# The last block's feed-forward network takes x times the norm weight with two shift columns, and applies the root mean square behind the products

## The reference

```
x   = x + g1x * y_x
hx2 = _modulate(_rms_norm(x, norm2_g[l]), sh2x, sc2x)      # x*rsqrt(mean x^2)*g*(1+sc) + sh
a, val = _split(hx2 @ w_up, (2816, 2816))
a   = conv_3x3(a as an image of 4 rows x 64 columns, each channel by itself, 'SAME') + conv_b
x   = x + g2x * ((gelu(a) * val) @ w_down)
out = rms_norm(x, final_norm_g)
```

## Time and profile before

| | us |
|---|---|
| median of 3 runs | 1181.13 (1180.99 to 1182.02) |
| the profiled execution's own time | 1182.99 |
| its span, first to last instruction | 1181.7 |
| PE busy | 1149.7 (97%) |
| DVE busy | 832.6 (70%) |
| ACT busy | 617.5 (52%) |
| POOL busy | 149.0 (13%) |
| mean granted clock of PE | 0.988 of 2.4 GHz |

### The profile page before, as it was taken

One profiled execution on the slowest core, in us unless ns is written; L12 is line 12 of the kernel. 1 busy time (PEld: TensorE's weight loads), 2 busy tenths in 40 slices (PEclk: granted clock), 3 DMA queues, 4 the chain that ended last, 5 costly groups with the idle time before them and its releaser, 6 DMA issues.

```text
span 1181.7 us, 21814 instructions
## 1 busy us (share of the span) xinstructions
PE 1149.7 (97%) x8998; PEld 1103.4 (93%) x8998; DVE 832.6 (70%) x1291; ACT 617.5 (52%) x933; POOL 149.0 (13%) x111
## 2 busy tenths in 40 slices
PE   7999899999999999999999999999999989999996
PEld 6989899999998899999999798988999979999995
DVE  5767588878685766777777775677546767767775
ACT  5655544445566645444444754755447455555553
POOL 0002101010100002100100000000000032444441
PEclk9999999999999999999999999999999989999998
DMA  8645478776534344888888545354235543555540
GB/s 313 230 144 178 155 245 295 242 258 197 164 122 160 125 161 134 289 289 270 283 264 274 198 128 172 120 166 161 92 107 176 180 161 126 179 182 178 193 143 36
DMA packets 60322, 221.36 MB, mean 187 GB/s; under 512 B 6736, under 2 KB 6992, under 8 KB 59840
## 3 DMA queue, kind: packets, MB, share of 16 engines
q1 hardware_dynamic: 59760, 218.53, 55.6%
q10 hardware_dynamic: 288, 1.05, 0.3%
q0 software_dynamic: 176, 0.39, 0.1%
HBM read 218.90 MB, written 1.05 MB: 186 GB/s over the span
## 4 chain that ended last, share of the span: by engine, by line
PE 90%; DVE 5%; ACT 3%; issue 1%; DMA 1%; SPq 0%; POOL 0%; ACTq 0%; DVEq 0%
PE PS L359 25%; PE PS L361 24%; PE PS L360 24%; PE PS L364 15%; ACT w_hi L850 2%; DVE w_lo L1330 1%; DVE PS L1928 1%; DMA ARENA<-memT 1%; DVE H_lo L1373 0%; PE PS L613 0%; ACT ARENA L947 0%; DVE SQ L1363 0%; DVE ARENA L1956 0%; DVE ARENA L1363 0%; DVE ARENA L1432 0%
## 5 line engine op out<-in xcount | busy, mean ns | idle before, releaser
L1330 DVE TENSOR_TENSOR w_lo<-raw,w_hi 128x1024 fp32r<-128x1024 f32 x325 | 398.1, 1227 | 176.5 <-ACT w_hi L850 175.8
L850 ACT ACTIVATE w_hi<-raw 128x1024 fp32r<-128x1024 f32 x356 | 371.9, 1054 | 149.3 <-PE PS L361 123.3
L359 PE MATMUL PS<-Y_hi,w_hi 128*128 128x256 f32 x1240 | 358.6, 289 | 9.9 <-DVE Y_lo L1369 3.2
L360 PE MATMUL PS<-Y_lo,w_hi 128*128 128x256 f32 x1240 | 353.9, 285 | 0.0
L361 PE MATMUL PS<-Y_hi,w_lo 128*128 128x256 f32 x1240 | 353.6, 285 | 0.0
L359 PEld LDWEIGHTS PS<-Y_hi,w_hi 128*128 128x128 f32 x1240 | 239.3, 193 | 17.2 <-issue 8.5
L360 PEld LDWEIGHTS PS<-Y_lo,w_hi 128*128 128x128 f32 x1240 | 239.9, 193 | 0.4 <-issue 0.2
L361 PEld LDWEIGHTS PS<-Y_hi,w_lo 128*128 128x128 f32 x1240 | 239.7, 193 | 0.0
L359 PE MATMUL PS<-H_hi,w_hi 128*128 128x256 f32 x768 | 220.2, 287 | 3.4 <-issue 1.0
L360 PE MATMUL PS<-H_lo,w_hi 128*128 128x256 f32 x768 | 217.3, 283 | 0.0
L361 PE MATMUL PS<-H_hi,w_lo 128*128 128x256 f32 x768 | 217.2, 283 | 0.0
(11 more groups left out here) (233 smaller groups left out, 1361.4 us busy)
## 6 DMA issues: line engine op xcount, KB each, us to landing
raw<-stream SPq DMA_DIRECT2D x404, 512.0 KB, 4.2
ARENA<-memT SPq DMA_DIRECT2D x2, 512.0 KB, 7.6
X<-xT SPq DMA_DIRECT2D x1, 1024.0 KB, 11.3
ARENA<-ctxT SPq DMA_DIRECT2D x1, 1024.0 KB, 5.8
ARENA<-memT SPq DMA_DIRECT2D x1, 1024.0 KB, 7.4
outT<-ARENA SPq DMA_DIRECT2D x2, 512.0 KB, 2.6
CROW<-c_rows SPq DMA_DIRECT2D x1, 512.0 KB, 10.0
ARENA<-c_rows SPq DMA_DIRECT2D x1, 512.0 KB, 13.2
```

Source lines behind the costliest of these rows:

```text
L359: pe.matmul(o, wh, xh, start=start, stop=False, skip_group_check=True)
L360: pe.matmul(o, wh, xl, start=False, stop=False, skip_group_check=True)
L850: act.activation(w_hi[n % RING][:], raw[at][:], ACT.Copy).then_inc(*mark("hi", n))
L1330: dve.tensor_tensor(w_lo[n % RING][:], raw[raw_of("slot", n)][:], w_hi[n % RING][:], ALU.subtract).then_inc(*mark("lo_dve", n))
```

## The change

- The pair (X times gain) is now written during w_o2, into new tiles U_hi and U_lo of 8 chunks x 258 columns, which lie in memory that other tiles of the arena used earlier. Columns 256 and 257 of each chunk hold the shift sh, split into hi and lo before w_o2 begins (`shift_hi`, `shift_lo`).
- Gate and up products of the last block are 258 columns wide. Column 256 is sh @ W.
- `residual_sum(2)` moves from between w_o2 and gate(0) into gate(0), ahead of its chunk 6. The normed pair H2 of this place goes (8 times L1363, L883, L1369).
- A new DVE step `scaled(j, i)` multiplies each gate (i = 0) and up (i = 1) product by RS in place and copies the shift's product from column 256 into a column SHIFTED. The image is written by Identity with that column as bias. `conv_mid` reads the image in place of PSUM. `conv_value` becomes (product + column) * gelu in one instruction.
- The order on ACT becomes: gelu of j-1; `img`, `conv_mid` of j; `hidden` of j-1; the fills. On DVE: `scaled(j, 0)`; `conv_value` of j-1; taps of j; `hidden_low` of j-1; fill; `scaled(j, 1)`; fill; third fill.
- The zeroing of the images moves ahead of w_o2.

```diff
-            project("w_o2", KC, Y2, ...)
-            residual_sum(2)
+            pe.wait_ge(*past("shift_lo"))
+            conv_gate_up(0, [("h_lo", 2, k) for k in range(KC)], lambda: residual_sum(2))
...
-                tall(PS[:, 2 * p, 0:T], H2, ready)
+                tall(PS[:, 2 * p, 0:T + 2], (U_hi, U_lo), ready, within)
...
-                tall(PS[:, 2 * p + 1, 0:T], H2)
+                tall(PS[:, 2 * p + 1, 0:T + 2], (U_hi, U_lo))
```

On ACT:

```diff
-            project("w_o2", KC, left, then=residual_square(2))
+            act.wait_ge(*past("gs", 2))
+            act.wait_ge(*past("mod", 3))
+            act.activation(U_hi[:, :, T:T + 2], SH2_COLS, ACT.Copy).then_inc(*mark("shift_hi"))
+            project("w_o2", KC, left, then=residual_square(2, U_TOKENS, lambda c: GS[:, 2, c:c + 1]))
             inverse_rms("res2")
-            whole(norm_his("norm2", H2, lambda c: SH2(c)))
             act.preload_act_table(ACT.Gelu)
...
                 act.wait_ge(*past("used", gate_slot(2, j)))
+                act.wait_ge(*past("scaled", j, 0))
+                act.wait_ge(*past("bias", j, 0))
                 act.wait_ge(*past("taps", j - 2, 7) if j > 1 else past("img_zero"))
-                act.activation(IMGS[:, j % 2, 1:ROWS + 1, 1:COLS + 1], img, ACT.Copy).then_inc(*mark("img", j))
-                act.activation(conv_sum(j), img, ACT.Identity, bias=gain("fconv_b", j),
+                act.activation(inner, img, ACT.Identity, bias=bias).then_inc(*mark("img", j))
+                act.wait_ge(*past("img", j))
+                act.activation(conv_sum(j), inner, ACT.Identity, bias=gain("fconv_b", j),
...
             for j in range(FC):
+                if j:
+                    conv_value(j - 1)
                 conv_gate(j)
                 if j:
-                    conv_value(j - 1)
+                    hidden(2, j - 1)
                 fill()
                 fill()
-                if j:
-                    hidden(2, j - 1)
```

On DVE:

```diff
-            project("w_o2", KC, residual(2, lambda c: G1(c)))
+            dve.memset(IMGS, 0.0).then_inc(*mark("img_zero"))
...
+            dve.tensor_tensor(U_lo[:, :, T:T + 2], SH2_COLS, U_hi[:, :, T:T + 2],
+                              ALU.subtract).then_inc(*mark("shift_lo"))
+            project("w_o2", KC, residual(2, lambda c: G1(c)),
+                    then=residual_low(2, U_TOKENS, lambda c: GS[:, 2, c:c + 1]))
+
+            def scaled(j, i):
+                half = PS[:, 2 * (j % 2) + i, 0:T]
+                dve.wait_ge(*past("used", gate_slot(2, j) + i))
+                dve.tensor_tensor(half, half, RS[:, 0], ALU.mult).then_inc(*mark("scaled", j, i))
+                at = 2 * i + j % 2
+                dve.tensor_copy(SHIFTED[:, at:at + 1], PS[:, 2 * (j % 2) + i, T:T + 1]).then_inc(*mark("bias", j, i))
...
-                dve.tensor_tensor(up_product(j), PS[:, 2 * (j % 2) + 1, 0:T], GF[:],
-                                  ALU.mult).then_inc(*mark("hidden", 2, j))
+                dve.scalar_tensor_tensor(up_product(j), PS[:, 2 * (j % 2) + 1, 0:T],
+                                         SHIFTED[:, 2 + j % 2:3 + j % 2], GF[:], ALU.add,
+                                         ALU.mult).then_inc(*mark("hidden", 2, j))
+            dve.wait_ge(*past("rs", "res2"))
             for j in range(FC):
+                scaled(j, 0)
                 if j:
                     conv_value(j - 1)
-                fill()
                 conv_taps(j)
-                fill()
                 if j:
                     hidden_low(2, j - 1)
+                fill()
+                scaled(j, 1)
+                fill()
```

More of the change, by code:

```diff
@@ L107 @@
     "conv_act": ("img", "conv_mid"),
+    "shift_dve": ("shift_lo", "scaled", "bias"),
     "gates_act": ("vs_gelu", "u_gelu", "sig_r", "sig_a", "sig_b"),
@@ L234, in build @@
         CX = (CX_hi, CX_lo)
-        sb("above", [P, 24832 - 19584])
+        U_lo, U_hi = sb("U_lo", [P, KC, T + 2], F32R), sb("U_hi", [P, KC, T + 2], F32R)
+        sb("above", [P, 24832 - 19584 - 2 * KC * (T + 2)])
         def area(at, *shape):
@@ L290, in build @@
         RS_COLS = small[:, 32:34]
+        SHIFTED = small[:, 0:4]
+        SH2_COLS = MOD[:, 24:32, 0:1].to_broadcast([P, KC, 2])
+        U_TOKENS = (U_hi[:, :, 0:T], U_lo[:, :, 0:T])
         RS_OF = {"mem0": RS[:, 1], "mix0": RS[:, 0], "mix1": RS[:, 0], "ctx": LR[:, 1], "out": RS[:, 0]}
@@ L813, in pe_program, with conv_gate_up @@
             project("w_o2", KC, Y2, lambda i: ("added", 2, i), None, [("merged_lo", i) for i in range(KC)])
-            residual_sum(2)
-            def conv_gate_up(j, ready=None):
+            def conv_gate_up(j, ready=None, within=None):
                 p = j % 2
@@ L1291, in conv_gate @@
                 img = PS[:, b, 0:T].rearrange("p (r c) -> p r c", r=ROWS)
+                inner = IMGS[:, j % 2, 1:ROWS + 1, 1:COLS + 1]
+                bias = SHIFTED[:, j % 2:j % 2 + 1]
                 act.wait_ge(*past("used", gate_slot(2, j)))
+                act.wait_ge(*past("scaled", j, 0))
+                act.wait_ge(*past("bias", j, 0))
                 act.wait_ge(*past("taps", j - 2, 7) if j > 1 else past("img_zero"))
-                act.activation(IMGS[:, j % 2, 1:ROWS + 1, 1:COLS + 1], img, ACT.Copy).then_inc(*mark("img", j))
-                act.activation(conv_sum(j), img, ACT.Identity, bias=gain("fconv_b", j),
+                act.activation(inner, img, ACT.Identity, bias=bias).then_inc(*mark("img", j))
+                act.wait_ge(*past("img", j))
+                act.activation(conv_sum(j), inner, ACT.Identity, bias=gain("fconv_b", j),
                                scale=gain("fconv", j + 4 * FC)).then_inc(*mark("conv_mid", j))
@@ L1916, in dve_program @@
             project("br_b", KC, branch_b, then=merged_low)
-            project("w_o2", KC, residual(2, lambda c: G1(c)))
+            dve.memset(IMGS, 0.0).then_inc(*mark("img_zero"))
             dve.wait_ge(*past("gs", 2))
-            whole(norms("norm2", X, lambda c: GS[:, 2, c:c + 1], ("res2", RS[:, 0]), H2, lambda c: SH2(c)))
-            dve.memset(IMGS, 0.0).then_inc(*mark("img_zero"))
+            dve.wait_ge(*past("mod", 3))
+            dve.wait_ge(*past("shift_hi"))
+            dve.tensor_tensor(U_lo[:, :, T:T + 2], SH2_COLS, U_hi[:, :, T:T + 2],
[8 more added lines that the diff above has]
+                dve.tensor_copy(SHIFTED[:, at:at + 1], PS[:, 2 * (j % 2) + i, T:T + 1]).then_inc(*mark("bias", j, i))
             def conv_taps(j):
@@ L1933, in conv_value @@
                 dve.wait_ge(*past("gelu", j))
-                dve.wait_ge(*past("used", up_slot(2, j)))
-                dve.tensor_tensor(up_product(j), PS[:, 2 * (j % 2) + 1, 0:T], GF[:],
-                                  ALU.mult).then_inc(*mark("hidden", 2, j))
+                dve.wait_ge(*past("bias", j, 1))
+                dve.wait_ge(*past("scaled", j, 1))
+                dve.scalar_tensor_tensor(up_product(j), PS[:, 2 * (j % 2) + 1, 0:T],
+                                         SHIFTED[:, 2 + j % 2:3 + j % 2], GF[:], ALU.add,
+                                         ALU.mult).then_inc(*mark("hidden", 2, j))
+            dve.wait_ge(*past("rs", "res2"))
             for j in range(FC):
+                scaled(j, 0)
                 if j:
                     conv_value(j - 1)
-                fill()
                 conv_taps(j)
-                fill()
                 if j:
                     hidden_low(2, j - 1)
+                fill()
+                scaled(j, 1)
+                fill()
                 if j > 1:
```

1 line of the change is left out of this document (removed).

## The result

The changed kernel takes 1184.09 us (median of 15 runs, 1182.2 to 1186.2), the kernel before 1181.13 us (15 runs, 1180.65 to 1183.07). The ratio is 1.0024 with a 95% interval of 1.0017 to 1.0031: about 3 us slower, where 1173.8 us and a gain of 7.3 were predicted. The profiled execution of the changed kernel took 1182.2 us and is the fastest of its 15, that of before took 1182.99 and is above its median. So in the two traces the changed kernel is the faster one by 0.8 us, 3.75 us away from what the medians say, and I compare stretches within a trace, not spans (1180.9 and 1181.7 us).

The account below looks back on a forecast made before the run. PE's rate was taken to bound the last stage, with the start of up(2) deciding. The terms -8.33 + 0.83 + 0.17 = -7.3 us took 1181.13 to 1173.8 us, range 1171.5 to 1177.2.

Parts of the forecast that it names:

- The passage from w_o2 into ffn2: From the end of w_o2 to up(2): up(2) starts at 982.10 in place of 990.43, 8.33 us sooner.
- The table load: Gelu table load before turn 0's image: 1.30 us by the row; a page drain of 1.38 would cut the gain 1.4.
- The stall at up(2) stays and the clock falls: At up(2), PE still stalls 3.06 us for the low part of G(0); the lower clock again costs 1.38 us.
- The clock stays up in the stall: Rival, 12%: the clock does not fall at the up(2) stall, 1.4 us less, 1172.4 us.
- So it holds, with 1.0 us to spare in a pair: Even flow of ffn2: 16.3 us of DVE work in a pair of turns that lasts PE 17.4 us.
- VectorE becomes the bound: Rival, 10%: in ffn2, dearer DVE work and fills beside POOL's make a pair 0.4 us longer: 3.8 us, 1177.6 us.
- My price from the row of layer 1: Within the VectorE rival: a DVE instruction on two SBUF tiles takes 0.96 us beside POOL instead of 0.48.
- Wider matmuls, +0.83 us: Gate and up products from up(2) on: two extra columns cost 0.9 ns a matmul over 39 slots of 24, +0.83 us.
- The end, +0.17 us: Last turn: down(20) waits for turn 20's low part behind taps starting at T + 1.85, before T + 1.68: +0.17 us.

Follow-up runs that it names:

- the collision taken away: Changed kernel with POOL's share of the last block's weight low parts left out, all but 8 of 1024 columns: 1172.56 us, ratio 0.9927.
- POOL alone: Changed kernel with all low parts of the last block from its fifth slot on made by POOL, none by DVE: 1170.67 us, ratio 0.9910.

## Why the prediction was wrong

- **The passage from w_o2 into ffn2**: right. 8.0 us gained where 8.33 were worked out; addition, sum, root, `img` and both sets of taps came within 0.1 to 0.3 us of their forecast places. The difference is one DVE fill of 1.38 in place of 1.23 us, which POOL held, and some 0.12 us more in a turn: `img` starts 0.17 us behind the copied column and not 0.04. Image and centre tap together took as long as forecast (0.48 and 0.57 us for 0.53 each).
- **The table load**: right by the row. `img` starts 0.02 us behind it. The drain of 1.38 us of the Trainium skill (ScalarE: Activation LUTs, "What ACT_TABLE_LOAD costs") is not in this trace either.
- **The stall at up(2) stays and the clock falls**: right. It fell 1.4 us after the restart, between 982.21 and 982.41, and not with it. The 24 matmuls of up(2) took 4.40 us (981.02 to 985.42) in place of 2.88, 1.5 us lost. *The clock stays up in the stall* did not happen in this trace, but in one of the variants it did, behind 2.01 us; what decides between the two stays open.
- **"So it holds, with 1.0 us to spare in a pair"**: this step failed. I put 16.3 us of DVE work into a pair of turns, with the fills at 1.14 us each, and a wait for POOL in the odd turn at nothing; the pair is 18.24. Of the 1.9 us between, 1.6 are the odd turn's fill, 2.73 us to the next instruction where I had 1.14; 0.2 are the later start of `img` and 0.1 the even turn's first fill. PE's own time for a pair is 17.25 us and not 17.4, so that 0.9 were to spare. With the collision taken away the rest fits (1172.56 us, and 0.5 us behind up(2) where I had 1.0).
- **"VectorE becomes the bound"**: the mechanism of this rival is what happened, at 10% and with 1.4 us a pair where 1.9 was true. By its own arithmetic, 1.8 eats up the gain. I looked at the lock of the Trainium skill (SBUF — State Buffer, "Who interferes with whom") in the even turn alone, and only for a DVE on time. There I put it at 0.4 us, and it took 0.1. In the odd turn POOL's third part follows `down(j-2)`, DVE's one fill follows the low part, and by my own times DVE is 0.5 us ahead. With POOL's parts nearly left out it was 0.11 to 0.12 us ahead; any lag above that turns their order round. In the changed kernel POOL had held an even turn's fill (1.37 us at 1006.25), and the next odd turn's came 0.05 us behind POOL. The trace agrees with the Trainium skill's rule that the later one waits for the whole of the other: 2.80 us where POOL had 1.72 left to run and the fill alone takes 1.22. My price from the row of layer 1 (0.96 in place of 0.48) was the same effect on a short instruction: in the changed kernel's w_o2, seven low parts of U with two SBUF inputs meet POOL's sum, and each ends 0.28 or 0.29 us behind it.
- **Wider matmuls, +0.83 us**: too much. The distance is the same for 256 and 258, and no difference in time can be told.
- **The end, +0.17 us**: too little. The stall ahead of down(20) was 0.40 us before, is 0.96 with the collision taken away, and 1.69 in the changed kernel, where DVE comes late to its last turns. So the 0.5 us behind up(2) are the end more than the width.

Together: -8.0 in the passage and +8.6 behind it is +0.6, nearly level; the 0.8 us by which the profiled execution is the shorter are these and 1.4 us that it was ahead at gate(0). The medians differ by 3.0, so some 2.4 us are not in the two traces. The changed kernel's median is 1.9 us above its profiled execution, and its 15 runs spread over 4.0 us where those of before spread over 2.4. Its mean granted clock is 0.997 in the fastest run and 0.991 in the two slowest. Whether the clock falls because the two engines meet more often in those runs, or for another reason, is not known.

## What to carry to other kernels

Where two engines that shut each other out of SBUF share a job in a loop, place their instructions in time against each other for each phase of the loop, and do it for an engine that is late, not only for one on time: free time in the sum of busy microseconds says nothing about it. If they can meet, give the whole job to the one that is idle, or make the idle one wait for the last of the busy one's; a wait behind the wrong instruction made it worse. And look for the low-priority result behind a long sequence (here a 0.4 us low part behind 4.2 us of taps): moved ahead, it took away the last stall, where POOL made all the low parts.

## What the runs showed of the hardware

- DVE's and POOL's `tensor_tensor` with two SBUF inputs exclude each other, and the one that comes first keeps its pace. DVE's took 2.80, 3.30 and 3.03 us when it started 0.68, 0.17 and 0.45 us behind a POOL one of 2.40 us, and 1.21 to 1.22 alone; it ended 1.08 or 1.09 us behind POOL's end each time. POOL's took 3.47 us 0.01 us behind a DVE one and 2.73 us 0.74 us behind it, in place of 2.40. DVE's taps and its low part of G, with one SBUF input, stayed at 0.49 and 0.42 us beside POOL.
- fp32r matmuls with 258 moving columns, in chunks 1032 bytes apart, start 0.1198 us apart, as those with 256; with 512 it was 0.23.
- The clock fell behind stalls of PE of 1.76 and 1.94 us, as behind those of 2.6 to 3.3, but not behind one of 2.01 us. It fell with the restart (before, 2.63 us) or 0.5 to 1.5 us later (0.5 with POOL's parts nearly left out, 1.4 in the changed kernel, 1.5 with POOL alone).
